# Attention in a hybrid decoder: value products of four row positions in one group instead of two

## The reference, cut to what matters

```python
def prompt_attend(q_lat, q_rope, ckv, krope):
    ...
        s = jnp.einsum('bqhr,bkr->bhqk', ql, ckv) + jnp.einsum('bqhd,bkd->bhqk', qr, krope)
        qpos = i * Q_BLOCK + jnp.arange(Q_BLOCK)
        s = jnp.where(kpos[None, :] <= qpos[:, None], s.astype(jnp.float32) * MLA_SCALE, NEG_INF)
        pr = jax.nn.softmax(s, axis=-1).astype(ckv.dtype)
        return jnp.einsum('bhqk,bkr->bqhr', pr, ckv)
```

## Time and profile before

| | us |
|---|---|
| runs (3): median | 3405.47 |
| runs: lowest, highest | 3404.98, 3409.25 |
| profiled execution, its own time | 3407.1 |
| span of the profiled execution | 3405.3 |
| PE busy in the span | 3307.9 |
| DVE busy | 2036.0 |
| ACT busy | 1272.5 |

### The profile page before, as it was taken

One profiled execution on the slowest core, in us unless ns is written; L12 is line 12 of the kernel. 1 busy time (PEld: TensorE's weight loads), 2 busy tenths in 40 slices (PEclk: granted clock), 3 DMA queues, 4 the chain that ended last, 5 costly groups with the idle time before them and its releaser, 6 DMA issues.

```text
span 3405.3 us, 88184 instructions
## 1 busy us (share of the span) xinstructions
PE 3307.9 (97%) x36916; PEld 2583.9 (76%) x36916; DVE 2036.0 (60%) x5230; ACT 1272.5 (37%) x3599; POOL 243.4 (7%) x284
## 2 busy tenths in 40 slices
PE   8999999999999999999999999999999999999998
PEld 6878786877868778697577787869777687776874
DVE  4656666665656646566356566666656565474653
ACT  3323333242343533434433233333423335234343
POOL 4200100000000000000050000000000000000000
PEclk9999999999999999999999999999999999999999
DMA  8654453627336163251375735436273351732512
GB/s 240 217 189 148 175 159 123 217 66 236 125 114 195 51 235 122 92 200 60 119 225 168 237 120 180 146 133 209 65 245 105 144 164 59 246 103 112 183 58 70
DMA packets 281055, 515.32 MB, mean 151 GB/s; under 512 B 30037, under 2 KB 215571, under 8 KB 268115
## 3 DMA queue, kind: packets, MB, share of 16 engines
q1 hardware_dynamic: 258903, 463.96, 41.4%
q0 software_dynamic: 11648, 41.95, 3.5%
q10 hardware_dynamic: 10108, 3.76, 0.4%
HBM read 473.15 MB, written 47.49 MB: 153 GB/s over the span
## 4 chain that ended last, share of the span: by engine, by line
PE 85%; DVE 7%; ACT 2%; issue 2%; DMA 2%; DVEq 1%; POOL 1%; ACTq 0%; POOLq 0%; SPq 0%
PE bank L828 78%; PE bank L832 8%; DVEq L1599 1%; DMA wout<-in_w_out 1%; DVE XX L1891 1%; DVE OO L1853 1%; DMA win<-in_w_in 1%; ACT PT L2768 1%; DVE Q L1811 0%; DVE XX L1894 0%; DVE qr L1812 0%; DVE X L1905 0%; DVE mix L1829 0%; ACT Sm L2722 0%; DVE Q L1814 0%
## 5 line engine op out<-in xcount | busy, mean ns | idle before, releaser
L828 PE MATMUL bank<-hT,win 64*64 64x256 f32 (+5 forms) x10224 | 1193.8, 352 | 5.9 <-DMA win<-in_w_in 2.5
L828 PEld LDWEIGHTS bank<-hT,win 64*64 64x64 f32 (+2 forms) x10224 | 957.2, 159 | 120.2 <-issue 36.4
L828 PE MATMUL bank<-wout,win 128*128 128x128 f32 x3136 | 379.9, 276 | 0.0
L828 PEld LDWEIGHTS bank<-wout,win 128*128 128x128 f32 x3136 | 364.6, 192 | 1.0
L828 PE MATMUL bank<-kv,Q 96*128 96x512 f32 (+3 forms) x640 | 277.5, 532 | 0.0
L1971 DVE TENSOR_REDUCE ml<-bank 128x1 f32<-128x512 f32 (+3 forms) x320 | 195.2, 610 | 124.3 <-PE bank L828 114.0
L832 PEld LDWEIGHTS bank<-cst,Sm 128*128 128x128 f32 x1344 | 157.6, 141 | 135.9 <-issue 72.2
L2722 ACT ACTIVATE Sm<-bank,ml 128x512 f32<-128x512 f32 (+3 forms) x320 | 200.0, 625 | 84.1 <-DVE ml L1976 76.2
L832 PE MATMUL bank<-cst,Sm 128*128 128x128 f32 x1344 | 210.7, 278 | 12.6 <-ACT PT L2572 5.9
L828 PE MATMUL bank<-wout,mix 128*128 128x512 f32 x480 | 215.1, 598 | 2.0 <-DMA wout<-in_w_out 1.1
L828 PEld LDWEIGHTS bank<-wout,mix 128*128 128x128 f32 x480 | 88.6, 190 | 107.5 <-issue 105.9
(11 more groups left out here) (529 smaller groups left out, 6028.8 us busy)
## 6 DMA issues: line engine op xcount, KB each, us to landing
win<-wfast SPq DMA_DIRECT2D x98, 1024.0 KB, 7.3
win<-in_w_in SPq DMA_DIRECT2D x78, 1024.0 KB, 5.7
win<-wfast SPq DMA_DIRECT2D x98, 768.0 KB, 6.4
wout<-in_w_out SPq DMA_DIRECT2D x60, 512.0 KB, 7.8
out_xres<-xin SPq DMA_DIRECT2D x16, 1024.0 KB
win<-in_w_in SPq DMA_DIRECT2D x16, 896.0 KB, 4.9
PT<-in_w_out SPq DMA_DIRECT2D x28, 512.0 KB, 4.4
XX<-in_w_out SPq DMA_DIRECT2D x28, 512.0 KB, 4.6
```

What stands on the lines that cost most here:

```text
L828: return pe.matmul(out, lhsT, rhs, start=start, stop=stop, skip_group_check=True)
```

## The change

Three edits. First, `group_of_values(m)` gives 4 for m = 1 to 3 and 2 for m = 0, and the values come in groups of that many positions, once every eight chunks (four for m = 0). Second, `PTo` gets eight places: the first four are now `Kt`, `Bp`, `sw` and `aa`, tiles that the recurrence has finished with by then; positions are numbered so that the last four of a block fall on the old places. `take` of an odd head waits for the position eight back. Third, ACT waits before the gate that writes `Kt` until all but the last four positions have been multiplied.

```diff
-        PTo = [PT[:, 0, :, :], PT[:, 1, :, :]] + [flat4(XX)[:, i * 512:(i + 1) * 512].rearrange("p (i t) -> p i t", i=4) for i in range(2)]
+        PTo = [t[:, :, :].rearrange("p a (b q) -> p (a b) q", b=2) for t in (Kt, Bp, sw, aa)] + [PT[:, 0, :, :], PT[:, 1, :, :]] \
+            + [flat4(XX)[:, i * 512:(i + 1) * 512].rearrange("p (i t) -> p i t", i=4) for i in range(2)]
...
+        def odd_probs(x, m):
+
+            return PTo[(x - 4 * (m + 1)) % 8]
+
+        def group_of_values(m):
+
+            return 4 if m else 2
...
-                n0, n = steps_before(l, m, e), 8 * (m + 1)
+                n0, n, G_ = steps_before(l, m, e), 8 * (m + 1), group_of_values(m)
...
-                    if c > m and (c - m) % 4 == 0:
-                        values((c - m) // 2 - 2)
-                        values((c - m) // 2 - 1)
-                for x in range((n - m - 1) // 4 * 2, n // 2):
+                    if c > m and (c - m) % (2 * G_) == 0:
+                        for x in range((c - m) // 2 - G_, (c - m) // 2):
+                            values(x)
+                for x in range((n - m - 1) // (2 * G_) * G_, n // 2):
                     values(x)
...
-                            if x >= 4:
-                                act.wait_ge(s_av.h, n0 // 2 + x - 3 + s_av.base)
-                            act.activation(PTo[x % 4][:, 0:k, :], PP[2 + c % 2][:, 0:k * P].rearrange("p (a t) -> p a t", a=k), ACT.Copy)\
+                            if x >= 8:
+                                act.wait_ge(s_av.h, n0 // 2 + x - 7 + s_av.base)
+                            act.activation(odd_probs(x, m)[:, 0:k, :], PP[2 + c % 2][:, 0:k * P].rearrange("p (a t) -> p a t", a=k), ACT.Copy)\
                                 .then_inc(s_ar[1].h, 1)
...
                     act.wait_ge(s_hs.h, s_hs.at(ip, 1))
+                    act.wait_ge(s_av.h, n0 // 2 + n // 2 - 4 + s_av.base)
                     gate(mix[:, 4:6, :], Kt)
```

More of the change, by code:

```diff
@@ L1235, in values @@
                     pe.wait_ge(s_ar[1].h, n0 // 2 + x + 1)
-                    even, odd = PTe[(2 * p + j) % 2][x % (m + 1)], PTo[x % 4]
+                    even, odd = PTe[(2 * p + j) % 2][x % (m + 1)], odd_probs(x, m)
                     k = chunk_width(B, c, m) // P
```

## The result

| | before | after |
|---|---|---|
| median of 13 runs each | 3409.24 | 3414.94 |
| lowest, highest | 3404.83, 3414.12 | 3410.75, 3421.18 |
| span of the profiled execution | 3405.3 | 3413.1 |
| forecast | | 3411.5, that is +6.0 on the 3405.5 of the first three runs |

The ratio is 1.0017, 95% interval 1.0009 to 1.0025: slower by 5.7 us (3 to 8.5), where the forecast was +6.0. That is a loss clear of no change, but a small one: it lies under the 0.2% that the forecast took as the border between same and slower. The absolute figure is 3.4 off, because the kernel before itself came out at 3409.2 over 13 runs, not 3405.5.

What follows compares the result with a forecast made beforehand. PE, 97% busy, bounds the kernel, so only its order and standstills count. Block terms sum to +2.98 us a layer, +6.0 for two, on 3405.5: 3411.5 us, range 3402 to 3416.

Steps and rivals of the forecast that it cites:

- The price of a group: On PE between scores and turn: entering, leaving and restarting around value products costs 0.31 us, late in a block 0.2.
- What the groups hid in m = 3: Blocks 6 and 7: removed groups uncover turns 8, 16, 24, which wait for exponentials; +2.29 and +1.43 us a layer.
- Block 6: First m = 3 block: turn(16) 1.02 late, turns 8 and 24 0.91 each, less group prices; +2.29 us a layer.
- Blocks 2 to 5: Blocks with m = 1 and 2: saved prices against uncovered ACT and DVE backlog; +0.09, -0.23, -0.03, -0.57 us a layer.
- block 4's first group: Block 4, turns 8 and 9: removing the group makes each 0.30 late; 0.79 with restarts and leftovers, less 0.31, +0.48 us.
- The upper bound of +1.1 a layer for blocks 2 to 5: Blocks 2 to 5 together: worst case, each first group as dear as in block 4; +1.1 us.
- (c): Rival: the narrow blocks lose more, each first group uncovering what block 4's does; +9.6 us, 3415.1, chance 0.23.
- The other edits: nothing: Eight places for odd copies and ACT's wait before the gate: PE is not held, no cost.
- (a): Rival: the cover isn't needed, only group prices go; -9.0 us, 3396.5, chance 0.09.
- (b): Rival: only m = 3 pays and the narrow blocks save in full; +2.1 us, 3407.6, chance 0.16.
- (d): Rival: the 12 new PE standstills each cost clock, 1.75 us apiece; +27 us, 3432, chance 0.02.
- The count of waits: PE's waits for exponentials in the profile after: near 40 and about 16 us, instead of 14 and 5.8.

Runs made afterwards that it cites:

- e6: The changed kernel, but each exponential waits only for its own chunk's maximum, with zero bias and a scale 64 times smaller; ratio 0.9970 against before.
- e5: The kernel before, but each exponential waits only for its own chunk's maximum, with zero bias and a scale 64 times smaller; ratio 0.9987 against before.
- e7: The changed kernel, but value groups of one position for m = 3 and of two for m = 1 and 2; ratio 1.0025 against before.
- e3: The changed kernel, but m = 3 groups moved to the other row starts, after chunks 7, 15, 23 and at the end; ratio 1.0035 against before.
- e11: The changed kernel, but for m = 2 and 3 DVE's eight scalings come after chunks 12 to 19 instead of 6 to 13; ratio 1.0015 against before.
- e1: The changed kernel, but groups of four for m = 1 and 2 only, m = 3 kept in twos; ratio 0.9992 against before.
- e4: The changed kernel, but groups of two for all m, leaving only the eight places and ACT's added wait; ratio 1.0002 against before.
- e9: The changed kernel, but in m = 3 scores(4r+3) are issued just ahead of turn(4r-2) instead of behind it; ratio 1.0007 against before.
- e10: The changed kernel, but m = 3 and block 2 in twos, blocks 3 to 5 regrouped, m = 3 scores(4r+3) issued before turn(4r-2); ratio 0.9992 against before.

## Why the prediction was right

- **The price of a group** (0.31). Right: 0.30 in block 7 by e6 less e5, and 0.30 by e7 once its standstill at turn(28) is taken off.
- **What the groups hid in m = 3.** Right in mechanism, place and size. Turn(8) 0.70 late (forecast 0.69), turn(16) 0.80 (0.80); e3 moved the gaps and e5 and e6 removed them by removing the wait for the row's maximum. Block 7 +1.46 against +1.43.
- **Block 6.** +2.75 and +2.48 against +2.29. Turns 8, 16 and 24 came as forecast (0.91, 1.01, 0.91 late). Two terms were mis-sized. Turn(4), which I had left as in before, was 1.13 and 1.12 late in the two layers against 0.80 and 1.05 before, 0.33 and 0.07 more. In layer 0 a scaling that waited for POOL held the maximum up on DVE (e11: 0.80 again, and the block 0.3 shorter). Without that the block is 2.42 and 2.41 longer. The 0.12 that is left over in both layers is the second small wait behind each uncovered turn: 0.32 in all by the starts, where I took 0.20.
- **Blocks 2 to 5.** Forecast -0.74 a layer, measured -1.05 and -0.55. Blocks 3 and 5 were right to 0.1. Block 2 varies by up to 0.8 between executions of the same order of work in it (-0.17 here, +0.61 in e1, +0.05 in e3), so that its agreement proves little. In block 5 turn(9) is 0.18 late, as forecast. In block 4 turns 8 and 9 are 0.23 and 0.34 late (0.30 each forecast), but turn(6), which I had left as in before, was 0.28 and 0.53 late instead of 0.60 and 0.75, and that hid part of the loss: here the sum came out close partly by luck. I had named the row maximum behind DVE's scalings as the cause of block 4's late turns; e11 gave 0.55 and 0.82 back when the scalings were moved.
- **Two sums.** The items of block 4's first group add to 0.82, not 0.79, which changes the forecast by less than 0.1 us. The upper bound of +1.1 a layer for blocks 2 to 5 doesn't follow from the figures printed with it (1.92 less 0.62, 0.38 and 0.16 is 0.76); it enters only case (c).
- **The other edits: nothing.** None seen (e4).
- **The rivals.** (a) fell: the prices alone are what is left only where the row maximum is out of the chain, and then they give 6.8 us and not 9.0. (b) fell with e1 and with the blocks of the changed kernel: the narrow blocks save 0.7 and 1.6 us in all, not 5.3. (c) fell too, as these blocks didn't lose; its +9.6 is also outside the 3 to 8.5 that was measured. (d) did not happen: the granted clock is 1.00 in blocks 6 and 7 of after, with 3.3 and 2.1 us of standstill in them and gaps of 0.6 to 1.1 us. The Trainium skill ("TensorE: Matmul & The Clock Gate", "A second HAM failure mode: psum-queue depth-cycling") tells of a kernel whose frequent short idles made the clock go back and forth; the trace does not show that here.
- **The count of waits.** I expected near 40 waits and 16 us; the profile had 30 and 14.8.

## What to carry to other kernels

Before work on the busiest engine is gathered into fewer and larger pieces, look what each piece stands in front of: a piece just ahead of an instruction that waits for another engine is a cover, and its overhead may be cheaper than the wait (here 0.30 against 0.70 to 1.01 us). The size of the wait can be read beforehand as the distance from the end of its last input to the waiting instruction, less the work that stays between, and a place in the same trace that already has no cover checks the sum. And a chain that is too long can be shortened: one matmul issued earlier, or another engine's side work moved off it. Grouping in m = 3 paid only where the wait for the row's maximum was out altogether (0.90 in block 7, e6 less e5). With the early scores alone it did not pay yet: block 7 came to -0.32 and 0.00 with groups of four (e9) and to -0.48 with groups of two (e10).

## What the runs showed of the hardware

From an exponential's end to the start of a transpose that stood waiting for it, it is 0.14 to 0.15 us in every kernel here, and a maximum starts 0.20 after the end of its scores wherever DVE stood ready (rows 6: 1587.32 to 1587.52). So the chain of three engines has the same length wherever nothing queues in it; the gaps computed from these for e3 came out within 0.01 us. Going from the full-width matmuls to a group of value products and back costs 0.30 us, in e6 less e5 and in e7. The profile shows this time as busy: in e7 PE's busy time grew by 2.16 us for seven further groups.
